# Two transformer blocks on one core: the last units of each stage by token tile or column half, with the next stage's norms, transposes and splits between their products

## What is computed

```python
# first block
hx = modulate(rms_norm(x, g_pre_mix), sh_m, sc_m)          # attention and retention over hx and the context
mix_x = merge_heads(att_x, ret_x, gr_x, w_out)
x_new = x + gt_m * rms_norm(mix_x, g_post_mix)
hf = modulate(rms_norm(x_new, g_pre_ffn), sh_f, sc_f)
x = x_new + gt_f * rms_norm(swiglu(hf, w_ffn_in, w_ffn_out), g_post_ffn)
# second block
x = x + 0.5 * swiglu_2(rms_norm_2(x, ffn1_norm), ffn1_gate, ffn1_up, ffn1_down)
z = rms_norm_2(x, mix_norm) @ w_in                          # gated linear recurrence and a short convolution
x = x + concat(y_hgrn, y_conv) @ w_out
qm = rms_norm_2(x, xattn_norm) @ w_q_mem                    # attention over 256 memory tokens
x = x + att @ w_o_mem
x = x + 0.5 * swiglu_2(rms_norm_2(x, ffn2_norm), ffn2_gate, ffn2_up, ffn2_down)
return rms_norm_2(x, final_norm)
```

## Time and profile before

| | |
|---|---|
| median of 3 runs | 1133.64 us (1132.88 to 1133.72) |
| the profiled execution | 1130.66 us, its span 1128.9 us |
| TensorE busy | 1044.4 us, 93% |
| VectorE, ScalarE busy | 598.6 us (53%), 491.1 us (44%) |
| HBM over the span | 167 GB/s |
| mean granted TensorE clock | 0.976 of full speed |

### The profile page before, as it was taken

The page is one execution under the profiler, slowest core; times in us unless marked ns, Lnnn a source line. Parts: engine busy times, 40 slices in busy tenths (PEclk is TensorE's granted clock), DMA queues, the critical chain, the costliest instruction groups (busy, mean ns, idle before and its releaser), DMA issues.

```text
span 1128.9 us, 13347 instructions
## 1 busy us (share of the span) xinstructions
PE 1044.4 (93%) x5212; PEld 843.3 (75%) x5212; DVE 598.6 (53%) x706; ACT 491.1 (44%) x581; POOL 0.2 (0%) x4
## 2 busy tenths in 40 slices
PE   4799999999699999989999999899889799999996
PEld 0478767777588887878888787688777577888785
DVE  1672854567565554455555545746654436555443
ACT  3353444445444444345444434653345336444431
POOL 0000000000000000000000000000000000000000
PEclk9799999999899999999999999899999999999998
DMA  9665653223255555536555455433224324555440
GB/s 374 266 254 224 238 212 146 75 75 112 75 187 186 186 186 182 191 112 239 182 187 179 163 192 211 167 132 112 79 107 151 112 75 186 187 186 186 169 167 37
DMA packets 26542, 188.71 MB, mean 167 GB/s; under 512 B 2944, under 2 KB 3200, under 8 KB 3968
## 3 DMA queue, kind: packets, MB, share of 16 engines
q1 hardware_dynamic: 25920, 185.63, 45.1%
q10 hardware_dynamic: 576, 2.43, 0.6%
HBM read 187.00 MB, written 1.05 MB: 167 GB/s over the span
## 4 chain that ended last, share of the span: by engine, by line
PE 86%; DVE 5%; ACT 3%; DMA 3%; issue 2%; SPq 0%; DVEq 0%; ACTq 0%
PE bank L1636 24%; PE bank L1638 24%; PE bank L1637 24%; DMA raw<-in_weights 3%; PE bank L1703 2%; PE bank L1692 1%; PE bank L1866 1%; PE bank L1974 1%; PE bank L1855 1%; DVE w_lo L1041 1%; ACT w_hi L577 1%; PE bank L2058 1%; PE bank L2157 1%; PE bank L2148 1%; PE bank L1903 1%
## 5 line engine op out<-in xcount | busy, mean ns | idle before, releaser
L1041 DVE TENSOR_TENSOR w_lo<-raw,w_hi 128x2048 fp32r<-128x2048 f32 (+1 forms) x153 | 339.2, 2221 | 334.3 <-ACT w_hi L577 334.1
L577 ACT ACTIVATE w_hi<-raw 128x2048 fp32r<-128x2048 f32 x148 | 282.8, 1915 | 382.3 <-PE bank L1638 353.0
L1636 PE MATMUL bank<-w_hi,hT_hi 128*128 128x512 f32 (+1 forms) x864 | 342.8, 397 | 12.2 <-DVE w_lo L1041 5.0
L1638 PE MATMUL bank<-w_hi,hT_lo 128*128 128x512 f32 (+1 forms) x864 | 336.7, 390 | 0.0
L1637 PE MATMUL bank<-w_lo,hT_hi 128*128 128x512 f32 (+1 forms) x864 | 336.6, 390 | 0.0
L1636 PEld LDWEIGHTS bank<-w_hi,hT_hi 128*128 128x128 f32 x864 | 163.5, 189 | 53.9 <-issue 10.1
L1638 PEld LDWEIGHTS bank<-w_hi,hT_lo 128*128 128x128 f32 x864 | 163.5, 189 | 34.5
L1637 PEld LDWEIGHTS bank<-w_lo,hT_hi 128*128 128x128 f32 x864 | 163.8, 190 | 31.9
L1636 PE MATMUL bank<-w_hi,gT_hi 128*128 128x512 f32 x264 | 103.7, 393 | 4.6 <-DVE arena L1438 4.6
L1638 PE MATMUL bank<-w_hi,gT_lo 128*128 128x512 f32 x264 | 102.8, 389 | 0.0
L1637 PE MATMUL bank<-w_lo,gT_hi 128*128 128x512 f32 x264 | 102.8, 389 | 0.0
(11 more groups left out here) (259 smaller groups left out, 1019.3 us busy)
## 6 DMA issues: line engine op xcount, KB each, us to landing
raw<-in_weights SPq DMA_DIRECT2D x172, 1024.0 KB, 4.8
arena<-in_const ACTq DMA_DIRECT2D x1, 1088.0 KB, 5.6
x_res<-in_x SPq DMA_DIRECT2D x1, 1024.0 KB, 8.2
arena<-in_ctx SPq DMA_DIRECT2D x1, 1024.0 KB, 9.9
memKT<-in_mem SPq DMA_DIRECT2D x1, 1024.0 KB, 10.3
out<-xn SPq DMA_DIRECT2D x2, 512.0 KB, 2.7
arena<-in_const SPq DMA_DIRECT2D x1, 770.0 KB, 6.2
rows<-in_final_norm ACTq DMA_DIRECT2D x1, 512.0 KB, 4.9
```

Source lines behind the costliest of these rows:

```text
L577: act.activation(w_hi[:, v_slot, :], raw[:, u_slot, :], ACT.Copy).then_inc(hi_ready, 1)
L1041: ins = dve.tensor_tensor(w_lo[:, v_slot, n], raw[:, u_slot, n], w_hi[:, v_slot, n].bitcast(F32), ALU.subtract)
L1636: pe.matmul(out, hi, rhi, start=start, stop=False)
L1638: return pe.matmul(out, lo, rhi, start=False, stop=stop)
```

## The change

The last units of a stage are done in another order, and the norm, transposes and splits of the next stage are put between their products. By stage:

- mixer to feed-forward 0, and feed-forward 0 to 1: by token tile. The last two units are done for tile 0, then for tile 1 (`tile0_done` marks the first). `post_norm` becomes `tile_stats`, `gained` and `add_gained` for one tile at a time, `four_transposes` becomes `tile_transposes` (four 128x128 slices of one tile in a bank). The next stage begins with tile 0 alone, for units W_UP, W_UP+1 and W_UP+2, then tile 1.
- feed-forward 1 to mix2T, mixer output to xattT, W_O to ffn2T: by column half. x is formed, transposed and split for one half while the other is in work; `pre_norm` does first one half, then the other. The last transposes stand within the next stage's first unit, between its token tiles. Halves of xattT come in the order 1, 0, and so do columns of `w_out_2` and halves of the first `w_q` columns in `lay_out`.
- feed-forward 2 to the final norm: by token tile.
- `unit` gets `release`, so that a slot is released only when both tiles have used it.

Cut to its core:

```diff
@@ plan_banks @@
+    def tile_transposes(stage, banks):
+        for tb in range(TB):
+            for half in range(2):
+                plan.signalled((stage, tb, half), banks[tb][half])
-    four_transposes("ffn0T")
+    tile_transposes("ffn0T", [[0, 2], [4, 5]])
-    four_transposes("ffn1T")
+    tile_transposes("ffn1T", [[4, 5], [6, 7]])
@@ ScalarE @@
+            def tile_stats(tb, src, ready):
+                for c in range(2):
+                    ready(c)
+                    act.activation(xn[:, tb, c * 512:(c + 1) * 512], src(c), ACT.Square,
+                                   accum_out=half_ss[:, c, tb:tb + 1]).then_inc(sem(f"tile_ss{c}"), 1)
...
+                act.activation(row_rms[:, tb:tb + 1], half_ss[:, 1, tb:tb + 1], ACT.Sqrt, scale=1.0 / D,
+                               bias=half_mean[:, tb:tb + 1]).then_inc(sem("tile_rms"), 1)
-            def pre_norm(stage, ready, gain, following):
+            def pre_norm(stage, ready, gain, following, first=0):
+                split_to(following + 1)
+                split_T(stage, gain, qs=[2 * first, 2 * first + 1])
                 split_to(following + 2)
-                split_T(stage, gain)
+                split_T(stage, gain, qs=[2 - 2 * first, 3 - 2 * first])
                 norm_stats(x, ready)
                 split_to(following + 3)
+            for tb in range(TB):
+                post_stats(("mix_out",), tb)
+                if tb:
+                    split_tile("ffn0T", 0)
+                    split_to(W_UP[0] + 2)
+                x_stats(("mix_out",), tb)
+                act.wait_ge(sem("tile_rstd"), stats[0])
+                act.activation(xn[:, tb, :], x[:, tb, :], ACT.Copy, scale=row_rstd[:, tb:tb + 1]).then_inc(sem("xn_tile"), 1)
+            split_to(W_UP[0] + 3)
+            split_tile("ffn0T", 1)
             ffn(0)
+            split_to(W_UP[1] + 1)
+            post_stats(("down", 0), 0)
             split_to(W_UP[1] + 2)
+            split_tile("ffn1T", 0, col("ffn1_norm"))
+            post_stats(("down", 0), 1)
+            split_to(W_UP[1] + 3)
+            split_tile("ffn1T", 1, col("ffn1_norm"))
+            norm_stats(x, x_added(("down", 0), 0))
@@ VectorE @@
+            def pre_norm(stage, name, gain, following, scale=None, first=0):
+                add_to_x(name, first, scale)
+                low_to(following + 1)
+                split_T(stage, gain, qs=[2 * first, 2 * first + 1])
+                add_to_x(name, 1 - first, scale)
                 low_to(following + 2)
-                norm_stats(x, ready)
+                split_T(stage, gain, qs=[2 - 2 * first, 3 - 2 * first])
+                norm_stats(x, x_added(name, 1))
                 low_to(following + 3)
+            for tb in range(TB):
+                gained(y_mix, ("mix_out",), 0, tb)
+                if tb:
+                    split_tile("ffn0T", 0, shift=(a_ffn, mod[:, 24:32, 0]))
+                    low_to(W_UP[0] + 2)
+                tile_rstd(tb)
+                add_gained(y_mix, ("mix_out",), tb)
+                tile_mean(tb)
+                tile_rstd(tb)
+            low_to(W_UP[0] + 3)
+            split_tile("ffn0T", 1, shift=(a_ffn, mod[:, 24:32, 0]))
@@ TensorE @@
-            mix_out(1, 0)
-            mix_out(1, 1)
+            mix_out(1, 0, [0], None)
+            mix_out(1, 1, [0], sem("tile0_done"))
+            mix_out(1, 0, [1])
+            mix_out(1, 1, [1])
@@ ffn: start @@
+                up_free(0, fills(0))
+                if f == 2:
+                    input_ready(stage)(0)
+                    up_unit(0, 0, up + 1, range(TB), before={1: lambda: transpose_x(stage, ("mem_out",), 1)})
...
+                else:
+                    tile_ready(stage, 0)
+                    up_unit(0, 0, up + 1, [0], None)
+                    up_unit(0, 1, up + 2, [0], None)
+                    second_tile()
+                    up_free(1, fills(1))
+                    up_unit(1, 0, up + 3, [0], None)
+                    tile_ready(stage, 1)
+                    up_unit(0, 0, up + 1, [1])
+                    up_unit(0, 1, up + 2, [1])
+                    up_unit(1, 0, up + 3, [1])
+                up_unit(1, 1, up + 4, range(TB))
@@ ffn: end @@
+                if f == 1:
+                    down(UP - 2, halves=[0], release=None)
+                    down(UP - 1, halves=[0], release=sem("down_half"))
+                    down(UP - 2, halves=[1])
+                    transpose_x("mix2T", ("down", 1), 0)
+                    down(UP - 1, halves=[1])
+                else:
+                    down(UP - 2, [0], release=None)
+                    down(UP - 1, [0], release=sem("tile0_done"))
+                    down(UP - 2, [1])
+                    down(UP - 1, [1], es=[0], release=None)
+                    if f == 0:
+                        next_tile(0)
+                    down(UP - 1, [1], es=[1])
```

More of the change, by code:

```diff
@@ new lines, in split_tile @@
+            def split_tile(stage, tb, gain=None):
+                t = slice(tb * P, (tb + 1) * P)
+                for half in range(2):
+                    if gain is None:
+                        act.wait_ge(sem("full_T"), shifts[0] + 1)
+                        act.activation(hT_hi[:, 4 * half:4 * half + 4, t], tile_buf(shifts[0]), ACT.Copy).then_inc(sem("T_hi"), 1)
+                        shifts[0] += 1
+                        continue
+                    b = filled(act, (stage, tb, half))
+                    for i in range(4):
+                        k = 4 * half + i
+                        ins = act.activation(hT_hi[:, k, t], b[:, i * P:(i + 1) * P], ACT.Copy, scale=gain[:, k:k + 1])
+                    ins.then_inc(sem("T_hi"), 1)
@@ L1106, in shifted_T_parts, with split_T @@
                 low(first + len(parts) - 1, *parts[-1])
-            def split_T(stage, gain=None, shift=None, hi=hT_hi, lo=hT_lo, n=4, first=0):
-                if shift is not None:
-                    shifted_T_parts([((stage, q), shift, hi, lo) for q in range(n)])
-                    return
-                for q in range(n):
+            def split_T(stage, gain=None, hi=hT_hi, lo=hT_lo, n=4, qs=None, first=0):
+                for q in qs or range(n):
                     name = (stage, q)
@@ L1591, in _ @@
             split_T("mix2oT", n=2)
[L1592 to L1594 removed]
+            low_to(W_OUT2 + 4)
+            pre_norm("xattT", ("mix2_out",), col("xattn_norm"), W_Q, first=1)
             low_to(W_O + 2)
@@ L1638, in three, with unit @@
                 return pe.matmul(out, lo, rhi, start=False, stop=stop)
-            def unit(v, ready, tiles, ks, n, first, last, before={}):
+            def unit(v, ready, tiles, ks, n, first, last, before={}, release=split_used):
                 pe.wait_ge(split_ready, ready)
@@ L2005, in down @@
-                    ins.then_inc(split_used, 1)
+                    for tb in tbs:
+                        for e in es:
+                            for half in halves:
+                                t = slice(tb * P, (tb + 1) * P)
+                                o = free(pe, ("down", f, tb, half)) if k == 0 and e == 0 else bank_of(("down", f, tb, half))
+                                w = slice(e * D + half * 512, e * D + half * 512 + 512)
+                                ins = three(o[:, :], gT_hi[:, 2 * k + e, t], gT_lo[:, 2 * k + e, t], w_hi[:, s, w], w_lo[:, s, w],
+                                            k == 0 and e == 0, k == UP - 1 and e == 1)
@@ new lines, in normed_tile, with next_tile @@
+            def normed_tile(tb):
+                pe.wait_ge(sem("xn_tile"), tb + 1)
+                transpose_tile("ffn0T", xn, tb)
+            def next_tile(tb):
+                for c in range(2):
+                    read_out(pe, ("down", 0, tb, c))
+                transpose_tile("ffn1T", x, tb)
+            normed_tile(0)
+            ffn(0, "ffn0T", lambda: normed_tile(1))
+            ffn(1, "ffn1T", lambda: next_tile(1))
+            z = lambda k, part: project(W_IN2 + 2 * k, [(part, 0), (part, 1)], ready=input_ready("mix2T") if k == 0 else None,
+                                        before={0: {1: lambda: transpose_x("mix2T", ("down", 1), 1)}} if k == 0 else {})
@@ L2128, in _ @@
                 read_out(pe, ("mix2oT", q))
-            mix2_out(0, 0)
             mix2_out(0, 1)
-            transpose_x("xattT", added(("mix2_out",)))
-            project(W_Q, [("mq", tb, 0) for tb in range(TB)], ready=input_ready("xattT"))
+            mix2_out(0, 0, {1: lambda: transpose_x("xattT", ("mix2_out",), 1)})
+            project(W_Q, [("mq", tb, 0) for tb in range(TB)], halves=(1, 0), ready=input_ready("xattT"),
+                    before={0: {1: lambda: transpose_x("xattT", ("mix2_out",), 0)}})
             def mem_queries(c):
```

297 lines of the change are left out of this document (163 added, 134 removed).

## The result

The changed kernel takes 1141.56 us (median of five runs, 1140.4 to 1143.32), 1.0068 times the kernel before, 95% interval 1.0054 to 1.0082. Slower was right, the size was not: +7.9 us against the forecast +4.0, and 1 us above the range. The profiled execution took 1140.4 us, its span 1138.6 us, at the same mean granted clock of 0.976.

A forecast was written before the change was run, and what follows sets the result against it. TensorE, busy 93% of the span, was taken as the bound, so only its standstills at six places could pay. Their terms sum to +4.0 us: 1130.66 becomes 1134.7, and 1137.6 us as a median; range 1131.5 to 1140.5.

The forecast's parts named there:

- B3: Feed-forward 1 to mix2T: splits behind constant loads delay the first product and the clock falls, +5.6 us (+3.85 to +6.3).
- B4: Second mixer's output to the memory queries (xattT): first products wait for half 0's sum, +0.4 us (0 to +0.6).
- B5: W_O to feed-forward 2: gate's transposes at 955.3 instead of 954.77, +0.5 us (0 to +1).
- B1: Mixer output to feed-forward 0: first product waits for tile 1's x, clock falls, +1.2 us (+0.4 to +3).
- B2: Feed-forward 0 to 1: gate's transposes at 525.7 instead of 527.60, -1.9 us (-2.6 to -0.5).
- B6: The end: tile 0 finished early, one scaling instead of two, -1.8 us (-1.4 to -2.3).
- R3: Rival: clock also falls in B2's gaps or a shorter one at B1, up to 2.3 us a fall; 1139.9 us, chance 0.10.
- R1: Rival: clock stays up at B1 and B3, or is back at once; +1.45 us, 1135.1 us, chance 0.14.
- R2: Rival: mix2T's half 0 splits before its loads, B1's bank is free; -2.65 us, 1131.0 us, chance 0.12.

The follow-up runs named there:

- the spacer dropped: Changed kernel without the 64-byte spacer `gap` ahead of gT_hi, so gT lies where it lay before: 1136.79 us, ratio 1.0030 to the kernel before.
- the spacer alone in the kernel before: Kernel before with the spacer ahead of gT_hi 64 bytes longer and nothing else changed: ratio 1.0032.
- w and hT moved: Changed kernel with its 64-byte spacer moved from ahead of gT_hi to ahead of w_hi: ratio 1.0028 to the kernel before.
- all together: Changed kernel without spacer, mix2T's constant loads behind its first split, third unit ahead of the norm's sums, new order at B1: 1126.2 us, 0.9930 of the kernel before.
- the loads moved: Changed kernel without spacer, three constant loads on ScalarE's queue behind mix2T's first two slices' split: 1132.16 us, 0.9977 of the kernel before.

## Why the prediction was wrong

- **The step that failed** is a sentence, not a term: "The products, weights and transposes are the same in number; only their order, the norms' pieces and the releases differ." I priced every product at the 0.227 us of the earlier trace rows, and never asked whether the two new tensors of the diff change anything. They cost 3.6 to 4.3 us: with the spacer dropped the ratio falls by 0.0038, and the spacer alone in the kernel before adds 0.0032. That is the whole miss, since the changed kernel at the old pace runs at 1136.8 us, 0.8 under the forecast. That the six terms came so near in sum (+4.0 forecast, +4.1 by the means) is in part luck: B3, B4 and B5 were 1.9 us short in all, and B1, B2 and B6 1.8 over.
- **B1** (+1.2): every time in it came out within 0.7 us (product 308.6, measured 308.08; gates' transposes 334.4, measured 334.40). Against the mean of four traces of before the step is only +0.2, since I had compared it with a lucky return of the clock. Over all five executions with the changed order at B1 and the old pace it is +0.6. Shift pieces: 0.34 us taken, eight take 2.64 us, a step of 0.32.
- **B2** (-1.9): the means give -2.5. ScalarE's eight pieces take 2.16 us, a step of 0.25 where I took 0.29. The estimate from the Trainium skill (VectorE: DVE Perf Modes, "The TRN2 errata") had been 0.25 us, so here its table was nearer to the step than my reading between rows; the single pieces are busy for 0.35 to 0.41 us. In the changed kernel the clock fell here (below), as it did in the run without the spacer, but not in the one with w and hT moved. I had taken 1.73 us as safe and 1.9 as safe enough; this fall is R3's, and it came, with 3.4 us at the lower level. At the old pace it cost 0.6 us and not R3's 2.3: from gates to gates lie 192.7 us in the two executions in which the clock fell here (no spacer; all together) and 192.1 in the six in which it stayed up. Those six wait 1.3 us for the `w_lo` of W_UP+2, and the fallen ones don't wait there.
- **B3** (+5.6): the mechanism is right in each part. The product waited on L1502 at 701.11; the forecast 698.65 with the 0.9 us of the second gates and 1.4 us of pace in this feed-forward makes 700.95; the clock fell; nothing was absorbed. The size was short by 1.4 us: the `w_hi` of W_IN2+2 lies 10.6 us behind the first product (700.06 to 710.68), not the 9.4 of my sum (698.65 to 708.05), since behind the splits ScalarE takes the norm's square first and then waits 1.2 us for VectorE's.
- **B4** (+0.4) came out at +0.7, **B6** (-1.8) at -2.0. **B5** (+0.5) came out at +0.7 in the means; the new wait of 1.46 us behind the norm's sums is the one that I had described there.

Windows of 1 us of the changed kernel; TensorE stood from 501.72 and resumed at 503.54:

```profile
503.00:504.00 1.00, 0.46 (x2) 0.45 (x3) 1.00 (x3) 0.00 (x0) 0.00 (x0) 1.00 0.00 0
504.00:505.00 1.00, 1.00 (x5) 0.76 (x4) 1.00 (x1) 0.00 (x0) 0.00 (x0) 0.53 0.00 0
...
507.00:508.00 1.00, 1.00 (x5) 0.75 (x4) 0.73 (x2) 1.00 (x2) 0.00 (x0) 0.76 0.45 180
```

The fall comes half a microsecond after the products are back. I had also overlooked one in the trace that I read: in the gap of 3.71 us at B2 the clock of the kernel before fell at 501.29, 3.1 us after the stop.

- R1 (the clock stays up) did not come at B1 and B3. R2 failed at its own point of decision: the split started behind the loads, at 697.7. Run with the loads moved, the part of R2 at B3 exists, at 0.9977.

## What to carry to other kernels

A new small tensor is a change to every tensor allocated behind it. Put the addresses of the two sides of a product into the comparison, and keep their distance a multiple of 256 bytes; if the pace between two products differs at equal clock, look there first. When work is put between products, list what stands ahead of it in each engine's queue, DMA issues and what they wait for included: the 3.6 us at mix2T, behind which the clock fell, were paid nearly twice. And take a place's price from several traces of equal programs before calling 1 us a result.
